# Delta rule: the next block's mixing opens a block, decay and rate products on row halves, a block's first weight products in one place

## The reference, cut to what matters

```
zs = z_rw + mu * (_time_shift(z_rw) - z_rw)                      # the mixing
r, kr, vr, wl, al, gl = _split(zs, [RWKV_WIDTH] * 3 + [DECAY_RANK, ICLR_RANK, GATE_RANK])
decay = jnp.exp(-jnp.exp(-jax.nn.softplus(-(w0 + jnp.tanh(wl) @ w2)) - 0.5))   # decay product
iclr = jax.nn.sigmoid(a0 + al @ a2)                                            # rate product
gate = jax.nn.sigmoid(gl) @ g2
kk = kr * k_k, per head divided by its norm;  kr = kr * (1.0 + (iclr - 1.0) * k_a)
S_t = S_{t-1} (diag(w_t) - kk_t^T (a_t * kk_t)) + v_t^T k_t ;  y_t = S_t r_t
y_rw = _head_norm(y_rw) * lnx_w + lnx_b;  out_rw = (y_rw + bonus) * gate
```

## Time and profile before

| | |
|---|---|
| median of 3 runs (lowest, highest) | 2434.14 us (2434.02, 2436.7) |
| the profiled execution: its time, its span | 2431.89 us, 2430.2 us |
| mean granted TensorE clock | 0.991 |
| PE busy | 2362.7 us (97%), 14214 matmuls |
| DVE busy | 1475.5 us (61%) |
| ACT busy | 1098.6 us (45%) |
| POOL busy | 237.5 us (10%) |
| the delta rule's eight blocks | 180.7 us to about 556 us |

### The profile page before, as it was taken

How to read it: one execution, slowest core, us unless ns; L and a number is a source line. 1 busy time by engine, 2 the same in 40 slices (tenths; PEclk the granted TensorE clock), 3 DMA queues, 4 the chain that set the end, 5 groups by cost and what they waited for, 6 DMA issues and landing times.

```text
span 2430.2 us, 36910 instructions
## 1 busy us (share of the span) xinstructions
PE 2362.7 (97%) x14214; PEld 1976.4 (81%) x14214; DVE 1475.5 (61%) x1645; ACT 1098.6 (45%) x1405; POOL 237.5 (10%) x184
## 2 busy tenths in 40 slices
PE   7999999999999999999999999989999999999997
PEld 7877777777888888888888888878888888888886
DVE  5456666765566466566566566775665565565664
ACT  5444444434544344344344445754543343343443
POOL 0002113421000000000000001220000000000001
PEclk9999999999999999999999999999999999999999
DMA  7653333333556666666666665556566566566654
GB/s 220 185 153 91 91 95 90 91 99 113 184 177 200 193 185 191 196 184 190 193 189 190 188 202 165 163 167 190 183 191 193 166 190 196 165 189 193 190 190 157
DMA packets 215464, 411.67 MB, mean 169 GB/s; under 512 B 13264, under 2 KB 19792, under 8 KB 215184
## 3 DMA queue, kind: packets, MB, share of 16 engines
q1 hardware_dynamic: 213888, 406.94, 54.5%
q0 software_dynamic: 1424, 2.49, 0.4%
HBM read 407.28 MB, written 2.10 MB: 168 GB/s over the span
## 4 chain that ended last, share of the span: by engine, by line
PE 92%; DVE 3%; issue 2%; ACT 2%; POOL 0%; DMA 0%; DVEq 0%; SPq 0%; ACTq 0%
PE acc_pair L226 19%; PE acc_pair L227 18%; PE acc_pair L228 18%; PE acc_pair L242 10%; PE tp_pair L242 10%; PE tp_pair L244 5%; PE acc_pair L244 5%; PE tp_pair L773 5%; PE acc_pair L773 1%; PE tp_pair L367 1%; DVE stg L724 1%; PE acc_pair L1569 1%; PE tp_pair L1569 1%; DVE w_lo L215 0%; ACT L766 0%
## 5 line engine op out<-in xcount | busy, mean ns | idle before, releaser
L215 DVE TENSOR_TENSOR w_lo<-raw,w_hi 128x1024 fp32r<-128x1024 f32 (+1 forms) x760 | 1014.8, 1339 | 764.3 <-ACT w_hi L210 758.0
L210 ACT ACTIVATE w_hi<-raw 128x1024 fp32r<-128x1024 f32 (+1 forms) x760 | 800.9, 1055 | 919.4 <-PE acc_pair L228 578.9
L242 PE MATMUL acc_pair<-xT_both,w_hi 128*128 128x512 f32 x1024 | 322.8, 397 | 12.1 <-issue 12.1
L242 PE MATMUL tp_pair<-xT_both,w_hi 128*128 128x512 f32 x1024 | 319.4, 393 | 0.0
L226 PE MATMUL acc_pair<-w_hi,xT_both 128*128 128x512 f32 (+1 forms) x736 | 301.9, 410 | 4.3 <-DVE w_lo L215 4.3
L227 PE MATMUL acc_pair<-w_lo,xT_both 128*128 128x512 f32 (+1 forms) x736 | 286.2, 389 | 0.0
L228 PE MATMUL acc_pair<-w_hi,xT_both 128*128 128x512 f32 (+1 forms) x736 | 285.9, 388 | 0.0
L226 PE MATMUL acc_pair<-w_hi,hidA_hi 128*128 128x512 f32 x640 | 251.9, 394 | 6.3 <-DVE hidA_lo L1603 6.3
L226 PE MATMUL acc_pair<-w_hi,hidB_hi 128*128 128x512 f32 x640 | 251.0, 392 | 0.0
L227 PE MATMUL acc_pair<-w_lo,hidA_hi 128*128 128x512 f32 x640 | 250.8, 392 | 0.0
L228 PE MATMUL acc_pair<-w_hi,hidA_lo 128*128 128x512 f32 x640 | 250.4, 391 | 0.0
(11 more groups left out here) (237 smaller groups left out, 2400.3 us busy)
## 6 DMA issues: line engine op xcount, KB each, us to landing
raw<-in_ff_w SPq DMA_DIRECT2D x512, 512.0 KB, 4.3
raw<-in_ev_w_in SPq DMA_DIRECT2D x112, 512.0 KB, 3.6
raw<-in_od_w_in SPq DMA_DIRECT2D x64, 512.0 KB, 4.2
raw<-in_ev_w_out SPq DMA_DIRECT2D x32, 512.0 KB, 3.6
raw<-in_od_w_out SPq DMA_DIRECT2D x32, 512.0 KB, 4.3
raw<-in_ev_w_in SPq DMA_DIRECT2D x8, 288.0 KB, 5.3
x<-in_x_in SPq DMA_DIRECT2D x4, 512.0 KB, 6.0
gate_w<-in_gx_w SPq DMA_DIRECT2D x8, 256.0 KB, 2.8
```

What stands on the lines that cost most here:

```text
L210: act.activation(w_hi[:, j % RING, :, 0:wide], raw[:, j % RING, :, 0:wide], ACT.Copy).then_inc(hi_ready, 1)
L215: dve.tensor_tensor(w_lo[:, j % RING, :, 0:wide], raw[:, j % RING, :, 0:wide], w_hi[:, j % RING, :, 0:wide], ALU.subtract).then_inc(lo_rea ...
L242: nc.tensor.matmul(o[:, :], w_hi[:, j % RING, kt % KU, c * P:(c + 1) * P], both, start=(kt == 0), stop=False)
```

## The change

Four things are done:

1. `dve_front_mix` of the next block moves from behind `split_lo` of unit 2 to the start of the block, ahead of everything else on DVE.
2. `split_lo` of unit 1 moves from the end of a block to the next block's start, behind the mixing (it is the same place in DVE's order but for the mixing).
3. `pe_front_lora` is replaced, within the blocks, by `pe_front_lora_heads`: four products of 64 rows by 64 columns over 256 tokens, so that only the 64 rows that hold something are used. The decay product goes to acc[1], the rate product to tp[3], and `act_front_tanh` reads the rate from there.
4. TensorE's order: 5 parts, first inverse product, variance, decay and rate products, instead of 3 parts, variance, first inverse product, 2 parts, decay and rate products.

```diff
+        def pe_front_lora_heads(pe, q):
+
+            pe.wait_ge(sem("front_lora_landed"), 32 * (q + 1))
+            pe.wait_ge(sem("tanh_ready"), 2 * q)
+            for m in (slice(0, CHUNK), slice(CHUNK, P)):
+                mm(acc[1][m, 0:T], lora_w[0:CHUNK, 0, m], lora_in[0:CHUNK, 0, :])
+                last = mm(tp[3][m, 0:T], lora_w[CHUNK:P, 0, m], lora_in[CHUNK:P, 1, :])
+            last.then_inc(sem("lora_done"), 1)
@@ rwkv_dve
+            if front:
+                dve_front_mix(dve, q)
             if norm:
+                split_lo(dve, g, 1)
                 dve_centre(dve, p - 1)
                 dve.wait_ge(sem("state_ready"), 3 * p)
...
             split_lo(dve, g, 2)
-            if front:
-                dve_front_mix(dve, q)
...
             else:
                 split_lo(dve, g + 1, 0)
-            split_lo(dve, g + 1, 1)
+                split_lo(dve, g + 1, 1)
@@ rwkv_pe
-            more(pe, p, parts, 3)
-            if norm:
-                pe_variance(pe, p - 1)
+            more(pe, p, parts, 5)
             pe.wait_ge(sem("inv_start"), p + 1)
             pe.wait_ge(sem("tokens_ready"), 2 * p + 2)
             for c in range(NCHUNK):
                 last = mm_heads(chunks(tp[1][:, 0:T])[:, c, :], inv_t[:, c, :], eye)
             last.then_inc(sem("inv_done"), 1)
-            more(pe, p, parts, 2)
+            if norm:
+                pe_variance(pe, p - 1)
             if front:
-                pe_front_lora(pe, p + 1)
+                pe_front_lora_heads(pe, p + 1)
```

More of the change, by code:

```diff
@@ L748, in act_front_square, with act_front_tanh @@
             act.activation(b_t, z_at(q, K_BLOCK), ACT.Square, scale=pcol_at("k_k", q)).then_inc(sem("kk_square"), 1)
-        def act_front_tanh(act, q, bank=acc[1]):
+        def act_front_tanh(act, q, bank=acc[1], rate=tp[3][:, 0:T]):
             act.wait_ge(sem("lora_done"), q + 1)
@@ L754, in act_front_tanh @@
                            bias=half_bias[:, 0, bass.ds(q, 1)]).then_inc(sem("tanh_ready"), 1)
-            act.activation(iclr_t, bank[:, T:2 * T], ACT.Tanh, scale=0.5,
+            act.activation(iclr_t, rate, ACT.Tanh, scale=0.5,
                            bias=half_bias[:, 1, bass.ds(q, 1)]).then_inc(sem("tanh_ready"), 1)
@@ L1135, in first_front @@
                     split_hi(eng, RET_N, 0)
-                    act_front_tanh(eng, 0, acc[3])
+                    act_front_tanh(eng, 0, acc[3], acc[3][:, T:2 * T])
                     act_front_exp(eng, 0)
```

## The result

The changed kernel takes 2407.45 us (median of 4 runs, 2406.72 to 2409.38), the kernel before in the same job 2434.65 (4 runs, 2434.02 to 2436.7). The ratio is 0.9888, 95% interval 0.9876 to 0.9901: a gain of 27.2 us, more than twice the 10.3 of the forecast's sum, and outside its range. The profiled run took 2406.72 us.

A forecast was written before the change was run, and what follows sets the result against it. TensorE, busy 97% of the span, was taken as the bound, with 7.9 us of waits for w_inv. 5.07 + 3.75 + 1.5 = 10.3 us off 2434.14 gave 2423.8 us; range 2420.5 to 2431.5.

The forecast's parts named there:

- Edit 1: Mixing moved to DVE's idle time at the block's start: frees TensorE's wait for w_inv in blocks 4 to 6, 5.07 us.
- Block 0: First block: level 1's w_inv product comes 2.55 us earlier and the clock stays up, 1.20 us; together 3.75 us.
- Edit 2: w_lo of unit 1 on DVE keeps its place, since it waited for its w_hi: worth nothing.
- Edit 3: Decay and rate products on row halves: gain 0.90 - x = 0.25 us a block, 1.5 us in blocks 1 to 6.
- x: Time of the eight half-product instructions ahead of level 1: taken as 0.64 us, bounds 0.43 to 2.9.
- (b): Rival: quarters sharing rows or columns run one after the other, 1.72 us a block; 2431.0 us in all; chance 0.11.
- (c): Rival: each half product also drains and restarts the array, 2.9 us a block; 2439.3 us in all; chance 0.06.
- Edit 4: TensorE's new order with the variance later: worth nothing, with at least 1.2 us of cover, 0.6 in block 7.
- cover: Margin by which w_inv is ready before TensorE reaches level 1's product: at least 1.2 us; any excess paid in seven blocks.
- Rival (a): w_lo and w_inv behind the late variance bring back the waits of blocks 4 to 6; 2428.9 us; chance 0.10.
- the sum's last: Step carrying the delta rule's gain to the kernel's end: it arrives in full, with 2 us allowed for shifted low-clock stretches.

The follow-up runs named there:

- a4: Kernel before with only the mixing moved to the block's start and w_lo of unit 1 behind it: 2424.66 us, 0.9964.
- d1: Kernel before with only TensorE's new order (5 parts, inverse product, variance, decay and rate products): 2445.86 us, 1.0048.
- a3: Kernel before with only the decay and rate products on row halves, 56 more TensorE instructions: 2422.26 us, 0.9957.
- a2: Changed kernel with the row halves undone, decay and rate products full-row again: 2423.99 us, 0.9961.
- a1: Kernel before with eight idle semaphore increments on TensorE ahead of layer 1's perceptron loop: 2419.85 us, 0.9946.
- b2: Changed kernel with idle increments moving layer 1's loop head 200 instructions later, to 3 before its code block's end: 2420.41 us, 0.9944.
- b3: Changed kernel with idle increments moving layer 1's loop head 99 instructions later, to 104 before its code block's end: 2408.77 us, 0.9896.
- b4: Changed kernel with idle increments moving layer 1's loop head 185 instructions later, to 18 before its code block's end: 2413.24 us, 0.9915.
- d3: Changed kernel with the moves of the mixing and of w_lo of unit 1 undone, row halves and new order kept: 2432.21 us, 0.9993.
- e1: Kernel before with TensorE's side of both perceptron loops written out, so no jump back there: 2414.16 us, 0.9918.

## Why the prediction was right and wrong

**Edit 1, right.** Timeline of DVE in block 5 after:
```profile
404.46 0.43 DVE L742 TENSOR_TENSOR seen<-z,decay 128x256 f32<-128x256 f32 x1 [0.56 <-PE tp_pair L773]
405.28 0.42 DVE L638 TENSOR_TENSOR stg<-z 128x255 f32 x1 [0.39 <-DVE seen L742]
...
406.48 1.27 DVE L698 SCALAR_TENSOR_TENSOR z<-stg,par,z 128x256 f32 x3
409.75 1.23 DVE L215 TENSOR_TENSOR w_lo<-raw,w_hi 128x1024 fp32r<-128x1024 f32 x1 [2.00 <-ACT w_hi L210]
```
The mixing costs 2.47 us (2.4 forecast), lies in the idle time before w_lo, and leaves 2.00 spare (2.5 forecast; it starts 0.39 later, waiting for L742's result). The earlier trace rows had 5.25 for it beside POOL. a4 shows the 1.69 a block to the hundredth: 48.90 to 47.21.

**Block 0, right**, 3.71 against 3.75. After, PE:
```profile
184.15 0.59 PE L773 MATMUL tp_pair<-con,inv_t 64*64 64x64 f32 x13 [1.22 <-DVE inv_t L905]
...
186.59 0.68 PE L773 MATMUL tp_pair<-w_inv,inv_t 64*64 64x64 f32 x16 [0.52 <-DVE w_inv L915]
...
190.72 0.68 PE L773 MATMUL tp_pair<-w_inv,inv_t 64*64 64x64 f32 x16
```
With the 1.16 us by which this run began earlier, the product stands at 187.75 (forecast 187.7); the idle stretches are 1.22 and 0.52 (1.1 and 0.5). Two small errors cancel on the way: the first inverse product starts at 185.31 (forecast 185.15), and the row halves behind it are shorter by as much. At the end the next product follows 4.13 later, the full-clock distance of the earlier trace rows.

**Edit 2, nothing**, as forecast (a4 holds it; its blocks are explained by edit 1 alone).

**Edit 3, right mechanism, wrong size.** Block 3 after:
```profile
322.29 1.38 PE L773 MATMUL acc_pair<-lora_in,lora_w 128*128 128x256 f32 x5
323.25 0.43 PE L773 MATMUL tp_pair<-lora_in,lora_w 64*64 64x256 f32 x1
323.25 0.43 PE L773 MATMUL acc_pair<-lora_in,lora_w 64*64 64x256 f32 x1
323.26 0.43 PE L773 MATMUL tp_pair<-lora_in,lora_w 64*64 64x256 f32 x1
323.51 0.38 PE L773 MATMUL acc_pair<-lora_in,lora_w 64*64 64x256 f32 x1
...
323.72 0.64 PE L773 MATMUL tp_pair<-inv,level_a 64*64 64x64 f32 x16
```
The first of the eight instructions is the last of the five in the first row (its own start is 323.24). One instruction of each quarter starts within 0.02 us, the second ones 0.26 later. So x is 323.72 - 323.24 = 0.48: all four quarters together, against the 0.64 taken. The blocks gained 0.45 instead of 0.25, 0.16 of it from x and 0.04 not resolved (0.08 if the restart after small tiles is taken as its own rows give it, 1.51 - 6 x 0.22 = 0.19, and not as 0.15); six blocks make 1.2 us: the delta rule's 11.5 against 10.3. Rivals (b) and (c) are out. Of the two sentences of the Trainium skill that the prediction cites (TensorE: Matmul & The Clock Gate, Part 3), the length of packed tiles (0.45) was close; the other, that a weight load overlaps only with a different row group, would have given 0.9 and is not seen here: the third quarter shares the rows of the first and starts 0.013 us behind it, and the weight loads of all four second instructions begin between 323.30 and 323.32, while matmuls on the same rows run.

**Edit 4, "Nothing" holds, but only beside edit 1.** Block 5 after, DVE's `w_inv` and the product that waits for it:
```profile
416.86 0.42 DVE L834 TENSOR_SCALAR stg<-acc_pair 128x256 f32<-128x256 f32 x1 [2.70 <-PE acc_pair L773]
...
418.60 0.41 DVE L915 TENSOR_TENSOR w_inv<-con,tp_pair 128x256 f32<-128x256 f32 x1
```
```profile
420.11 0.68 PE L773 MATMUL tp_pair<-w_inv,inv_t 64*64 64x64 f32 x16
```
418.60 + 0.46 = 419.06, product at 420.11: 1.05 us of cover where 1.2 was worked out. Rival (a) is out. d1 shows the sentence "whatever exceeds the cover is paid in seven blocks" at work: with the mixing still behind the variance the cover is gone and 11.7 us are lost.

**The step that failed** is the sum's last: "What follows is full of TensorE's work again, so I expect it to arrive at the end; late in the run long waits are followed by a low clock, and the shift can change how these fall, which I allow 2 us for." It did arrive, but 12.8 us more came on top, out of a stretch that the sum put at nothing; the rest of the miss is x (1.2) and the scatter of start and runs. The prediction counted added matmuls only as time. They are also addresses: 56 instructions ahead of a loop moved its head from 3 before the end of a code block to 203 before the end of the next (a3 has the 56 without the other edits and a2 the other edits without them; a1, b2, b3 and b4 move the head by itself). Their sign was chance: b2 has every edit and 200 idle instructions, and gives 13.0 us back. The wait was readable beforehand: 12.1 us in four waits ended by "issue", more than the 7.9 that the forecast dealt with. That a small edit would remove it was not.

What stays open: why block 0 starts anywhere from 178.65 to 182.75 us in the profiled runs, why the branch of one and the same loop takes 3.3 us once and 4.8 another time, and why a wait of 1.60 or 2.00 us is followed by a low clock in one block and not in the next.

## What to carry to other kernels

Read the waits ended by "issue" behind a backward jump of a long loop before any other, and count where the loop's head lies in its 256 instructions: an edit anywhere ahead of it moves it, and a gain or a loss of 13 us can come from there, so time a change also with a few idle instructions added, or write the loop out on the engine that bounds. An edit that is worth nothing by itself (the order, 0.07 us a block) can cost 12 us without its companion: make the room first, then move work onto the edge of it. A time that doesn't change can hide two large effects, as in d3; only the ledger by stretch tells.

## What the runs showed of the hardware

- A jump back on TensorE in a loop of 1876 instructions takes 3.3 to 4.8 us, part of it hidden behind matmuls already issued. TensorE's idle time, over the two perceptron loops of all profiles, is 0.67 to 2.15 us (mostly about 1.0) with the loop's head 103 to 251 instructions before the end of its block; 0.69 to 0.88, then 2.41 to 2.43, at 18 (b4); and 4.48 to 5.48 at 3 (before, a2, a4, b2, d1), each time with 6.8 us at 1.2 GHz. The jump back of a short loop, of 441 instructions, took 0.24 us (before, at 98.07).
- The fetch behind the jump's own begins 1.2 to 2.8 us after the branch has ended, wherever in its block the head lies.
- Four 64x64 products of 256 columns in float32 on the four quarters take 0.48 us together, as long as one and a little; on the full array two products with half the rows empty took 0.86.
- A wait of 2.00 us (a3) went with 3.4 us at the low clock in blocks 4 and 5 and not in block 6; one of 1.61 us (before, blocks 4 to 6) did not; of the three of 1.60 and 1.61 us in e1 one did. Where the clock fell, the block took 1.3 to 1.5 us longer.
